# Stick-breaking attention's running sum: two rounded products, high part and rest, in place of one fp32 product

## The reference

```python
z = jnp.einsum('bhqd,bhkd->bhqk', qb, kt, preferred_element_type=jnp.float32)
log_fail = jnp.where(strict, jax.nn.log_sigmoid(-z), 0.0)
after = lax.cumsum(log_fail, axis=3, reverse=True) - log_fail
w = jnp.where(strict, jnp.exp(jax.nn.log_sigmoid(z) + after), 0.0)
return jnp.einsum('bhqk,bhkd->bhqd', w.astype(vt.dtype), vt)
```

## Time and profile before

| | |
|---|---|
| median of 3 runs | 3391.97 us (3391.57 to 3392.92) |
| the profiled execution's own time | 3391.2 us |
| its span, first to last instruction | 3389.4 us |
| TensorE busy | 3319.6 us, 98% |
| VectorE busy | 1966.8 us, 58% |
| ScalarE busy | 1653.5 us, 49% |
| GpSimd busy | 498.9 us, 15% |
| mean granted TensorE clock | 0.992 |
| SB steps | 16, one every 49.41 us in each layer |

### The profile page before, as it was taken

One profiled execution on the slowest core, in us unless ns is written; L12 is line 12 of the kernel. 1 busy time (PEld: TensorE's weight loads), 2 busy tenths in 40 slices (PEclk: granted clock), 3 DMA queues, 4 the chain that ended last, 5 costly groups with the idle time before them and its releaser, 6 DMA issues.

```text
span 3389.4 us, 48369 instructions
## 1 busy us (share of the span) xinstructions
PE 3319.6 (98%) x17528; PEld 2838.2 (84%) x17528; DVE 1966.8 (58%) x2190; ACT 1653.5 (49%) x2322; POOL 498.9 (15%) x425
## 2 busy tenths in 40 slices
PE   8999999999999999999999999999979999999998
PEld 7888888888888888888888888888869889898897
DVE  6666645444444556666545444445466776667755
ACT  5444555555444444444555554444335464545643
POOL 4554400000000104554200000000020000010000
PEclk9999999999999999999999999999989999999998
DMA  6555555555555555555554555555533334443342
GB/s 235 173 169 175 183 174 167 168 173 173 193 192 193 199 182 182 170 173 174 175 177 165 169 173 187 193 193 185 180 138 134 116 125 156 156 138 124 124 144 95
DMA packets 157148, 567.24 MB, mean 167 GB/s; under 512 B 17536, under 2 KB 19728, under 8 KB 156752
## 3 DMA queue, kind: packets, MB, share of 16 engines
q1 hardware_dynamic: 155680, 558.00, 49.0%
q0 software_dynamic: 1344, 7.49, 0.6%
HBM read 563.32 MB, written 2.10 MB: 167 GB/s over the span
## 4 chain that ended last, share of the span: by engine, by line
PE 95%; DVE 3%; ACT 1%; POOL 1%; issue 0%; DMA 0%; SPq 0%; ACTq 0%; DVEq 0%; POOLq 0%
PE acc L1506 22%; PE acc L1508 22%; PE acc L1507 22%; PE acc L1757 6%; PE acc L1759 6%; PE acc L1758 6%; PE work L1566 1%; DVE w_lo L965 1%; PE work L1592 1%; PE work L1835 1%; PE work L1836 1%; PE work L1806 1%; PE work L1736 1%; PE work L1737 1%; PE work L1738 1%
## 5 line engine op out<-in xcount | busy, mean ns | idle before, releaser
L965 DVE TENSOR_TENSOR w_lo<-raw,w_hi 128x1024 fp32r<-128x1024 f32 x1056 | 1401.3, 1336 | 1214.4 <-ACT w_hi L565 944.0
L565 ACT ACTIVATE w_hi<-raw 128x1024 fp32r<-128x1024 f32 x832 | 876.4, 1058 | 964.3 <-PE acc L1508 961.9
L1506 PE MATMUL acc<-w_hi,hT_hi 128*128 128x512 f32 x2560 | 1015.2, 397 | 2.3 <-DVE hT_lo L971 2.3
L1508 PE MATMUL acc<-w_hi,hT_lo 128*128 128x512 f32 x2560 | 998.9, 390 | 0.0
L1507 PE MATMUL acc<-w_lo,hT_hi 128*128 128x512 f32 x2560 | 997.5, 390 | 0.0
L1508 PEld LDWEIGHTS acc<-w_hi,hT_lo 128*128 128x128 f32 x2560 | 481.0, 188 | 102.7
L1506 PEld LDWEIGHTS acc<-w_hi,hT_hi 128*128 128x128 f32 x2560 | 481.5, 188 | 97.8 <-issue 2.7
L1507 PEld LDWEIGHTS acc<-w_lo,hT_hi 128*128 128x128 f32 x2560 | 481.8, 188 | 95.8
L579 ACT ACTIVATE w_hi<-raw 128x1024 fp32r<-128x1024 f32 x224 | 236.1, 1056 | 395.8 <-PE acc L1759 381.0
L1757 PE MATMUL acc<-h_hi,w_hi 128*128 128x272 f32 x1152 | 344.7, 299 | 0.0
L1759 PE MATMUL acc<-h_hi,w_lo 128*128 128x272 f32 x1152 | 333.2, 289 | 0.0
(11 more groups left out here) (311 smaller groups left out, 3738.7 us busy)
## 6 DMA issues: line engine op xcount, KB each, us to landing
raw<-weights SPq DMA_DIRECT2D x1056, 512.0 KB, 3.3
mat<-mats POOLq DMA_DIRECT2D x2, 1536.0 KB, 8.1
X<-x_in SPq DMA_DIRECT2D x8, 256.0 KB, 7.9
out<-out_rows SPq DMA_DIRECT2D x8, 256.0 KB, 2.3
par<-params POOLq DMA_DIRECT2D x2, 640.0 KB, 5.4
cst<-consts POOLq DMA_DIRECT2D x1, 872.0 KB, 5.0
cst<-consts POOLq DMA_DIRECT2D x1, 704.0 KB, 4.8
ropeC<-rope POOLq DMA_DIRECT2D x2, 256.0 KB, 5.6
```

The costliest lines, as they stand in the source:

```text
L565: act.activation(w_hi[:, slot, :], raw[:, slot, :], ACT.Copy).then_inc(hi_ready, 1)
L965: dve.tensor_tensor(w_lo[:, s % RING, :], raw[:, s % RING, :], w_hi[:, s % RING, :], ALU.subtract)\
L1506: pe.matmul(o, stat[0][:, kc, token], hi, start=(kc == 0), stop=False)
L1508: ins = pe.matmul(o, stat[1][:, kc, token], hi, start=False, stop=(kc == KC - 1))
```

## The change

The running sum becomes two rounded products. ScalarE makes `sm_hi`, the masked softplus rounded to fp32r, and VectorE makes `sm_lo`, the rest, in two new operations. They stand in the queues after ScalarE's s = 7 split and after VectorE's s = 8 split. `sm_hi` and `sm_lo` lie where `QN` and `SQ` do. The two matrices are copied once into a new fp32r tile `tri`, on ScalarE in the first step of layer 0. `cumulate` has four products of 384 columns and four of 128 in place of two and two. `sp_ready` is now raised by the subtraction that gives `sm_lo`; the mask raises `sp_sum` a second time.

```diff
+        sm_hi = mem.place("sm_hi", [P, 2, 384], F32R, at=qn_at)
+        sm_lo = mem.place("sm_lo", [P, 2, 384], F32R, at=sq_at)
...
+        tri = mem.place("tri", [P, 2 * P], F32R)
...
+                if l == 0:
+                    act.wait_ge(cst_loaded, 16)
+                    act.activation(tri[:, :], cst[:, C_NEGTRI:C_NEGTRI + 2 * P], ACT.Copy)
                 split(u, 14, 16)
...
+            def softplus_hi(m):
+
+                act.wait_ge(sp_sum, 2 * m["k"] + 2)
+                act.activation(sm_hi[:, :, :], SM[:, :, :], ACT.Copy).then_inc(sp_hi, 1)
...
-                split(u, 7, 10)
+                split(u, 7, 8)
+                if prev and prev["kind"] == "SB":
+                    softplus_hi(prev)
+                split(u, 8, 10)
...
-                dve.wait_ge(sp_sum, k + 1)
+                dve.wait_ge(sp_sum, 2 * k + 1)
                 keep = cst[:, C_SBKEEP:C_SBKEEP + 384].unsqueeze(1).to_broadcast([P, 2, 384])
-                dve.tensor_tensor(SM[:, :, :], SM[:, :, :], keep, ALU.mult).then_inc(sp_ready, 1)
+                dve.tensor_tensor(SM[:, :, :], SM[:, :, :], keep, ALU.mult).then_inc(sp_sum, 1)
+
+            def softplus_lo(m):
+
+                dve.wait_ge(sp_hi, m["k"] + 1)
+                dve.tensor_tensor(sm_lo[:, :, :], SM[:, :, :], sm_hi[:, :, :], ALU.subtract).then_inc(sp_ready, 1)
...
-                split(u, 8, 10)
+                split(u, 8, 9)
+                if prev and prev["kind"] == "SB":
+                    softplus_lo(prev)
+                split(u, 9, 10)
...
                 pe.wait_ge(sp_ready, m["k"] + 1)
                 for a in range(2):
-                    pe.matmul(work[:, 2 + a, 0:384], cst[:, C_NEGTRI:C_NEGTRI + P], SM[:, a, :], start=False, stop=True,
-                              skip_group_check=True)
-                    ins = pe.matmul(work[:, 2 + a, P:256], cst[:, C_NEGONE:C_NEGONE + P], SM[:, a, 256:384], start=False,
-                                    stop=True, skip_group_check=True)
+                    for part in (sm_hi, sm_lo):
+                        pe.matmul(work[:, 2 + a, 0:384], tri[:, 0:P], part[:, a, :], start=False, stop=True,
+                                  skip_group_check=True)
+                    for part in (sm_hi, sm_lo):
+                        ins = pe.matmul(work[:, 2 + a, P:256], tri[:, P:2 * P], part[:, a, 256:384], start=False,
+                                        stop=True, skip_group_check=True)
                 ins.then_inc(cumulated, 1)
```

More of the change, by code:

```diff
@@ L207, in build_program @@
         subln = mem.place("subln", [P, 256])
+        tri = mem.place("tri", [P, 2 * P], F32R)
+        assert mem.at <= 229376, mem.at
         x_loaded = sems("x_loaded", 8)
@@ L227, in build_program @@
             sem(n) for n in ("maxed", "probs", "mixing", "mixed", "aT_turned", "aT_copied"))
-        sp_steps, sp_ln, sp_sum, sp_ready, cumulated, w_arg, w_ready = (
-            sem(n) for n in ("sp_steps", "sp_ln", "sp_sum", "sp_ready", "cumulated", "w_arg", "w_ready"))
+        sp_steps, sp_ln, sp_sum, sp_hi, sp_ready, cumulated, w_arg, w_ready = (
+            sem(n) for n in ("sp_steps", "sp_ln", "sp_sum", "sp_hi", "sp_ready", "cumulated", "w_arg", "w_ready"))
         av_ready, o_sq, head_steps, o_rs, u_ready = (sem(n) for n in ("av_ready", "o_sq", "head_steps", "o_rs", "u_ready"))
```

## The result

| | before | changed |
|---|---|---|
| median | 3391.77 us (6 runs) | 3404.80 us (6 runs, 3403.74 to 3405.57) |
| ratio | | 1.0038, 95% interval 1.0025 to 1.0050 |
| profiled execution: own time, span | 3391.2, 3389.4 | 3405.57, 3403.8 |

The changed kernel is 13.0 us slower, where 11.5 was forecast (3403.5). In the changed kernel the lines are renumbered: ring products L1530 to L1532, ring splits L570 (ScalarE) and L981 (VectorE), mask L1066, sm_hi L672, sm_lo L1071, running sum L1617 (384 columns) and L1620 (128), argument of the exponential L1077, exponential L676.

What follows compares the result with a forecast made beforehand. TensorE, busy 98%, bounds the kernel. Per step +1.33 stall + 1.13 - 1.74 = +0.72 us, +11.5 over 16 steps, giving a 3403.5 us median from 3391.97; range 3397 to 3412.

Steps and rivals of the forecast that it cites:

- TensorE as the bound: TensorE is busy for 98% of the span; a microsecond taken from its queue, or spent waiting, counts a microsecond.
- stall: TensorE's wait for sm_lo at the running sum: first product at 466.35 instead of 465.02, 1.33 us a step, 16 times.
- The block of products: TensorE's running-sum products: 1.74 us a step before, 1.13 after (bounds 0.96 and 1.53), 0.61 less, 9.8 us in all.
- The chain: Mask's end, sm_hi, both s = 8 splits, then sm_lo on ScalarE and VectorE: from 462.21 to 466.17.
- The wake-up of TensorE: Delay from the end of VectorE's subtraction to TensorE's weight load at the running sum: 0.06 us.
- the 0.12: At the running sum, the first product starts 0.12 us after its weight load when a whole load is exposed.
- The cover behind the stall: Later splits, exponential and slot reloads stay hidden behind TensorE's ring: no cost; without cover, up to 2 us a step.
- 1 (no stall): At the running sum, s = 8 splits don't lie between sm_hi and sm_lo; no stall, 3382 us; chance 6%.
- 2 (dear products): Rounded 128-column running-sum products cost as much as fp32, 3410 us; 384-column ones too, 3440; together 12%.
- rival 3: TensorE's clock drops after each running-sum stall, two microseconds at the lower level: 16 us, 3420 us; chance 4%.
- 4 (absorbed by overlap): Queued operations overlap more, absorbing 0.3 us of stall a step: 3398 to 3399 us; chance 8%.
- The sum: Per step +1.33 stall, +1.13 new products, -1.74 old ones: +0.72 us; 16 steps give +11.5.

Runs made afterwards that it cites:

- experiment 2: Changed kernel with TensorE's running-sum products put back to full fp32, still waiting for sm_lo: 3413.42 us against 3391.76 for the kernel before, ratio 1.0063.
- the first experiment: Also experiment 1: changed kernel with VectorE making sm_lo ahead of its s = 8 split: 3382.44 us against 3391.76 for the kernel before, ratio 0.9972.
- experiment 4: Kernel with sm_lo ahead of the s = 8 split, with each step's four 128-column products left out: 3374.71 us against 3391.51 for the kernel before.
- experiment 6: Two kernels: the kernel before plus only the copy into tri, 3391.99 us against 3391.76; the changed kernel unedited, profiled again, 3404.54 us against 3391.51.
- experiment 5: Kernel with sm_lo ahead of the s = 8 split, with the subtraction done twice: 3385.74 us against 3391.51 for the kernel before, ratio 0.9984.

## Why the prediction was right, point by point

- TensorE as the bound: held. A microsecond of stall cost about one (experiment 2: 1.29 a step for 1.33), and a microsecond of product saved gave one (experiments 1 and 4).
- The block of products: 1.74 to 1.13. In the first experiment the steps are 0.62 shorter, forecast 0.61 (by the medians 9.3 / 16 = 0.58). The single prices, 0.173 and 0.11, were measured as 0.175 and 0.115. Taking the transposes' spacing for the unseen 128-column product was the choice that mattered; the bounds lay 3 us below and 6 above.
- The chain: mask to sm_lo 3.96 us, as added up. The wake-up of TensorE is 0.05 (467.76 to 467.81), forecast 0.06. One reading was slightly off: the trace stamps the product at the same moment as its weight load, not 0.12 later, and the 0.12 appears as the longer distance to the second product (467.81 to 468.10 is 0.29, not 0.17). The sum is the same. That the 0.12 came out right is partly luck: the load it was read from (L1849, 2647.45) isn't exposed. The product before it starts at 2647.44, and 0.13 later the next one is due in any case, by the spacing of the earlier trace rows. Where TensorE had waited, in the step of the earlier trace rows, product and load carry the same start, 2981.31:

```profile
2981.31 0.28 PE L1782 MATMUL work<-cst,PJ 128*16 128x128 f32 x1 [0.69 <-DVE K L1203]
```

- The cover behind the stall: held. No split is waited for in any of these kernels.
- The rivals: 1 (no stall) became true only when the order was changed, and then at 3382.44 for 3382. 2 (dear products) fell with experiment 4, for both sizes. 3 fell too: in the changed kernel the granted clock was 1.00 around the first stall (452 to 474) and over all eight steps of the first layer (452 to 862), where two microseconds at half the clock behind each of eight stalls would give 0.98. (Behind a wait of 2.15 us elsewhere the clock did fall in some executions; see experiment 6.)

```profile
452.00:474.00 22.00, 20.95 (x98) 17.32 (x97) 11.66 (x11) 14.53 (x16) 0.00 (x0) 1.00 0.44 144
...
452.00:862.00 410.00, 401.60 (x1894) 334.36 (x1893) 204.80 (x180) 222.54 (x249) 15.52 (x16) 1.00 0.51 168
```

  4 (absorbed by overlap) would have shown in the chain, which came out whole.
- The sum: +11.5 forecast, +13.0 measured, +11.1 and +14.4 in the two profiled spans. Per step 0.72 forecast, 0.72 and 0.71 in these, so the mechanism's share came out as added up. The last 1.5 us of the medians are outside the steps. The GpSimd waits in one of the two profiles and the granted clock behind the steps are two known sources of such differences; neither is shown to be the 1.5.

## What to carry to other kernels

A cheaper operation on the bounding engine is no gain until the chain that feeds it has been added up in queue order, with every foreign instruction that stands between its links: here two ring splits, themselves nowhere near due, put 2.1 us into a chain that takes 1.9 without them, against 2.6 us of cushion. When a new link is put on another engine, let it go ahead of work that nobody waits for, or let the consumer stand later in its queue; here either is worth 22 us or more, and the cheaper operation 9.9. The cushion, from the producer's end to the consumer's weight load, can be read from one step of the timeline before anything is built.

## What was not expected of the hardware

GpSimd and VectorE exclude one another in the differential steps, and which of them loses differs between executions (1.31 or 2.45 us for the same GpSimd product); in one of the two profiles of the changed kernel this made TensorE wait twice where the kernel before doesn't.

TensorE's clock does fall behind a wait, as rival 3 had it, but in other places and not in every execution: behind the same wait of 2.15 us, far behind the steps that were changed, it is 0.50 in the profiles of experiments 1 and 5 and 1.00 in that of the kernel before. In experiment 5 the executions with the lower mean clock took 2 us longer.
